# Two halves of a split weight, interleaved in one buffer instead of two buffers

## The chip, the cores and the metric

One core of a Trainium2 chip runs the whole program. The metric is the device time in microseconds, the median of several executions. TensorE multiplies, VectorE and ScalarE work element by element, GpSimd and SyncE here mostly issue transfers. A matmul on TensorE has a stationary operand, brought in by a separate weight load, and a moving operand that is streamed past it; both are read from SBUF, the on-chip memory of 128 partitions.

## What is computed

Two transformer blocks in a row on 256 positions of width 1024, all in fp32. The first has two kinds of attention and a gated feed-forward layer with a short convolution; the second has an attention layer and a gated convolution layer, each followed by a gated feed-forward layer. Cut to what matters here:

```python
# first block
h = rmsnorm(x, attn_norm_g[l]); proj = h @ w_in[l]
o_fox = fox_attention(...); o_sb = stick_breaking_attention(...)
x = x + o @ w_out[l]
h = rmsnorm(x, ffn_norm_g[l])
u = causal_dwconv(h @ w_up[l], conv_w[l], conv_b[l])
gate, val = jnp.split(u, 2, axis=-1)
x = x + (jax.nn.silu(gate) * val) @ w_down[l]
# second block, i = 0 and 1
mod = sc @ w_ada[i] + b_ada[i]
h = modulate(x, norm_mix[i], sh_m, sc_m)
y = moba_attention(h, w_qkv[j], w_o[j], ...) if i == 0 else short_conv(h, w_in[j], conv_w[j], w_out[j])
x = x + g_m[:, None, :] * y
h = modulate(x, norm_ffn[i], sh_f, sc_f)
x = x + g_f[:, None, :] * swiglu(h, w_gate_up[i], w_down[i])
```

Nearly all the arithmetic is in the products with weights: w_in, w_out, w_up, w_down, w_qkv_2, w_o_2, w_in_2, w_out_2 and two each of w_gate_up_2 and w_down_2.

## The kernel before

**Split products.** To keep fp32 accuracy with fast matmuls, every fp32 operand is split into two of type fp32r: an upper half (the rounded value) and a lower half (what the rounding left). A product is then three matmuls, in `products` (lines 1417, 1418, 1419): upper with upper, upper with lower, lower with upper.

**Chunks and units.** Weights arrive as 147 chunks of 1 MB (128 partitions x 2048 values), in a ring of four buffers `w_raw`, by transfers that SyncE issues. A chunk is two units of 128 x 1024 values (`UNIT`), 294 units in all. For each unit ScalarE copies the raw values to the upper half (`w_hi`, `split_unit`, line 505) and VectorE subtracts that from the raw values to give the lower half (`w_lo`, line 857). Both buffers are rings of `SPLIT` = 4 units. ScalarE may write unit u once TensorE is done with unit u - 4 (`unit_done`), VectorE once ScalarE is done (`hi_ready`), TensorE may use the unit once VectorE is done (`lo_ready`).

**Stages.** The chunks in order: IN1 (0 to 11), OUT1, UP1 (16 to 37), DOWN1 (38 to 48), QKV (49 to 60), OUT2, UP2 (65 to 86), DOWN2 (87 to 97), IN3 (98 to 109), OUT3, UP3 (114 to 135), DOWN3 (136 to 146). Between the units of IN1 and QKV stand the small matmuls of attention. UP and DOWN run mostly in hardware loops, and a loop of UP splits two chunks ahead, so the loop of UP3 also splits chunks 136 and 137.

**Which operand is stationary.** In most stages a 128 x 128 tile of the weights is stationary, and the activations (`act_hi`, `hid_hi`, `ot_hi`, ... with their lower halves) move, 256 columns at a time: a unit is 8 tiles, so 24 matmuls. In the chunks of the values (v) of both attentions, 2, 5, 10 and 11 of IN1 and 4, 7, 10 and 11 of QKV, the weights move, 256 columns at a time (`half_chunk` with `moving`). In DOWN3 (`down_tokens`) they move 512 columns at a time: a unit is 4 products, 12 matmuls.

**Beside the stream of weights**, VectorE adds up `ada_acc` (the product with w_ada_2, whose 48 MB come in over GpSimd's queue as `ada_raw`), does the convolutions, norms and residuals, and ScalarE does the activations. The order of work on each engine is written out by hand in the block of that engine; nothing reorders it.

Of the kernel before, what the change touches and what calls it, by code (L numbers as in the profile page):

```python
# [66 lines left out]

BANKS_DONE = {OUT1: 0, DOWN1: 1, OUT2: 4, DOWN2: 5, OUT3: 8, DOWN3: 9}
# [20 lines left out]
def model_kernel(nc, x, attn_norm_g, w_in, forget_bias, fox_out_g, sb_out_g, w_out, ffn_norm_g, w_up,  # L89
# [3 lines left out]
    with ctx:  # L93
# [8 lines left out]
        w_hi = sb("w_hi", [P, SPLIT, UNIT], F32R)  # L102
        w_lo = sb("w_lo", [P, SPLIT, UNIT], F32R)
# [224 lines left out]
        def unit(buf, u):  # L328
            return buf[:, u % SPLIT, :]
# [161 lines left out]
        def _(act):  # L491
# [5 lines left out]
            def split_unit(c, h, i=None):  # L497
                u = 2 * c + h
                if u == 0 and i is None:
                    act.wait_ge(w_first, 16)  # L500
                elif h == 0 or u == 1:
                    act.wait_ge(w_landed[c % RAW], at(16 * (c // RAW + 1), 16, i))
                if u >= SPLIT:
                    act.wait_ge(unit_done, at(u - SPLIT + 1, 8, i))
                act.activation(unit(w_hi, u), raw_half(c, h), ACT.Copy).then_inc(hi_ready, 1)  # L505
# [339 lines left out]
        def _(dve):  # L845
# [568 lines left out]
        def _(pe):  # L1414
# [6 lines left out]
            def half_chunk(c, h, dst, src_hi, src_lo, i=None, operand=None, moving=False):  # L1421
# [6 lines left out]
                whi, wlo = unit(w_hi, u), unit(w_lo, u)  # L1428
# [16 lines left out]
            def arriving(u, h, dst, src_hi, src_lo, operand):  # L1445

                for j in (2 * h, 2 * h + 1):
# [3 lines left out]
                    for k, t, w in tiles:  # L1451
                        o = dst[:, t * T:(t + 1) * T]
                        pe.matmul(o, unit(w_hi, u)[:, w], src_hi[:, k, :], start=k == 0 and t == 0, stop=False,  # L1453
                                  skip_group_check=True)
                        pe.matmul(o, unit(w_lo, u)[:, w], src_hi[:, k, :], start=False, stop=False, skip_group_check=True)  # L1455
                    pe.wait_ge(h_lo, 4 * operand + j + 1)
                    for k, t, w in tiles:
                        ins = pe.matmul(dst[:, t * T:(t + 1) * T], unit(w_hi, u)[:, w], src_lo[:, k, :], start=False,  # L1458
                                        stop=k == KT - 1, skip_group_check=True)
                ins.then_inc(unit_done, 1)  # L1460

            def first_half():
# [5 lines left out]
                for j in range(2):  # L1468
                    pe.wait_ge(h_hi, 2 * j + 2)
                    for k, t, o, w in tiles(j):  # L1470
                        pe.matmul(o, unit(w_hi, 0)[:, w], act_hi[:, k, :], start=k == 0 and t == 0, stop=False,
                                  skip_group_check=True)
                for j in range(2):
                    pe.wait_ge(h_lo, j + 1)
                    for k, t, o, w in tiles(j):
                        pe.matmul(o, unit(w_hi, 0)[:, w], act_lo[:, k, :], start=False, stop=False, skip_group_check=True)
                pe.wait_ge(lo_ready, 1)
                for j in range(2):
                    for k, t, o, w in tiles(j):
                        ins = pe.matmul(o, unit(w_lo, 0)[:, w], act_hi[:, k, :], start=False, stop=False,  # L1480
# [7 lines left out]
            def output_chunk(c0, n, h, k_hi, k_lo, ready=None):  # L1488
# [9 lines left out]
                for outputs in (range(4),) if n < 3 else (range(2), range(2, 4)):  # L1498
                    for r in tiles:
# [4 lines left out]
                        for o in outputs:  # L1504
                            w = slice(r % 2 * 2 * CW + o * P, r % 2 * 2 * CW + (o + 1) * P)
                            dst = bank[OUT_BANKS[c0][2 * (n % 2) + o // 2]][:, (o % 2) * T:(o % 2 + 1) * T]
                            ins = products(dst, unit(w_hi, w_unit)[:, w], unit(w_lo, w_unit)[:, w], k_hi(k), k_lo(k),
# [36 lines left out]
            def down_layer(c0, pair0):  # L1544
                def rows(d, i=None):
                    pe.wait_ge(hid_lo_r, at(pair0 + d + 1, 4, i))
                    for h in range(2):
# [3 lines left out]
                        for o in range(KT):  # L1551
                            w = slice(o * P, (o + 1) * P)
                            ins = products(bank[4 + o // 2][:, (o % 2) * T:(o % 2 + 1) * T], unit(w_hi, u)[:, w],
                                           unit(w_lo, u)[:, w], hid_hi[:, cols(kt, 8, i, 1), :], hid_lo[:, cols(kt, 8, i, 1), :],
# [10 lines left out]
                for j in range(4):  # L1565
                    for h in range(2):
                        u, kt = 2 * (c0 + 10) + h, 20 + h
                        for o in (2 * j, 2 * j + 1):
                            w = slice(o * P, (o + 1) * P)
                            ins = products(bank[4 + j][:, (o % 2) * T:(o % 2 + 1) * T], unit(w_hi, u)[:, w],  # L1570
                                           unit(w_lo, u)[:, w], hid_hi[:, kt, :], hid_lo[:, kt, :], False, h == 1)
# [381 lines left out]
```

## Time and profile before

| | before |
|---|---|
| median of the runs shown | 969.9 us (3 runs, 967.15 to 971.51) |
| profiled execution | 967.1 us, span of its profile 965.5 us, mean granted TensorE clock 0.996 |
| TensorE matmuls | 931.0 us busy, 7571 |
| TensorE weight loads | 904.0 us busy, 7571 |
| VectorE | 715.6 us busy |
| ScalarE | 482.4 us busy |
| GpSimd | 45.3 us busy |
| HBM read | 205.75 MB, 214 GB/s over the span |

Busy is the time in which an engine had an instruction under way. Matmuls are pipelined and their ends are modelled, so matmuls that follow each other overlap in the table, and a mean duration is longer than the time between two starts. Weight loads are listed as an engine of their own (PEld) and overlap the matmuls. Groups of instructions are named by line, engine, operation and by output and inputs: `bank<-act_hi,w_hi` has act_hi moving and w_hi stationary, `bank<-w_hi,act_hi` the other way round.

### The profile page before, as it was taken

The numbers are of one execution on the slowest core, as the hardware profiler recorded it, in microseconds if no ns is written. First come the engines' busy times: TensorE is split into PE (matmuls) and PEld (weight loads), VectorE is DVE, ScalarE is ACT, GpSimd is POOL, SyncE is SP. The second block draws the span as 40 slices with busy tenths as digits, with TensorE's granted clock in tenths as the row PEclk, the third lists the DMA queues.
The fourth block names the chain that finished last, engine by engine and source line by source line (L and its number), as shares of the span: only waits on it lengthen the run. The fifth ranks groups of instructions, "written<-read, shape, count | busy, mean of one in ns | idle before, by whom it ended". The sixth has DMA issues, their size and how long they took to land.

```text
span 965.5 us, 18807 instructions
## 1 busy us (share of the span) xinstructions
PE 931.0 (96%) x7571; PEld 904.0 (94%) x7571; DVE 715.6 (74%) x942; ACT 482.4 (50%) x704; POOL 45.3 (5%) x79
## 2 busy tenths in 40 slices
PE   7899899999999999999999999999999999999998
PEld 7899789999989999899999999999999999999886
DVE  6799757799999779988675777787867575555544
ACT  6345645566655336555464444534544454445541
POOL 4000000000010100001000001000000000000000
PEclk9999999999999999999999999999999999999999
DMA  9778332766767985566736788798465545656541
GB/s 296 236 270 316 113 129 69 240 217 218 228 253 286 382 289 175 177 216 220 240 114 212 253 278 297 266 367 282 134 210 181 175 131 183 209 176 208 173 140 44
DMA packets 130969, 207.61 MB, mean 215 GB/s; under 512 B 4582, under 2 KB 109408, under 8 KB 124768
## 3 DMA queue, kind: packets, MB, share of 16 engines
q1 hardware_dynamic: 122784, 156.43, 48.4%
q0 software_dynamic: 6912, 50.33, 14.5%
q8 instruction: 40, 0.66, 0.3%
q10 hardware_dynamic: 1216, 0.05, 0.1%
q14 instruction: 17, 0.14, 0.0%
HBM read 205.75 MB, written 1.05 MB: 214 GB/s over the span
## 4 chain that ended last, share of the span: by engine, by line
PE 64%; DVE 23%; ACT 4%; issue 4%; DMA 4%; ACTq 0%; POOL 0%; DVEq 0%; POOLq 0%
PE bank L1417 18%; PE bank L1418 18%; PE bank L1419 18%; DVE w_lo L857 8%; DVE ada_acc L872 4%; DVE conv L966 3%; DMA ada_raw<-in_w_ada 3%; ACT w_hi L505 2%; PE bank L1522 2%; PE bank L1458 1%; PE bank L1453 1%; PE bank L1455 1%; DVE hidden L979 1%; DVE scr L892 1%; PE bank L1637 1%
## 5 line engine op out<-in xcount | busy, mean ns | idle before, releaser
L857 DVE TENSOR_TENSOR w_lo<-w_raw,w_hi 128x1024 fp32r<-128x1024 f32 x294 | 354.0, 1223 | 152.9 <-ACT w_hi L505 149.7
L505 ACT ACTIVATE w_hi<-w_raw 128x1024 fp32r<-128x1024 f32 x294 | 306.0, 1055 | 250.3 <-PE bank L1419 240.8
L1417 PE MATMUL bank<-act_hi,w_hi 128*128 128x256 f32 x1440 | 401.3, 279 | 6.1 <-DVE w_lo L857 3.7
L1418 PE MATMUL bank<-act_lo,w_hi 128*128 128x256 f32 x1440 | 398.1, 276 | 0.0
L1419 PE MATMUL bank<-act_hi,w_lo 128*128 128x256 f32 x1440 | 398.1, 276 | 0.0
L1417 PEld LDWEIGHTS bank<-act_hi,w_hi 128*128 128x128 f32 x1440 | 270.4, 188 | 7.6 <-DVE w_lo L857 7.3
L1418 PEld LDWEIGHTS bank<-act_lo,w_hi 128*128 128x128 f32 x1440 | 270.5, 188 | 0.3 <-issue 0.2
L1419 PEld LDWEIGHTS bank<-act_hi,w_lo 128*128 128x128 f32 x1440 | 270.6, 188 | 0.0
L872 DVE SCALAR_TENSOR_TENSOR ada_acc<-ada_raw,silu_c,ada_acc 128x2048 f32<-128x2048 f32 x48 | 112.6, 2347 | 10.7 <-DMA ada_raw<-in_w_ada 10.7
L1417 PE MATMUL bank<-hid_hi,w_hi 128*128 (+1 forms) x352 | 98.2, 279 | 4.0 <-DVE w_lo L857 4.0
L1418 PE MATMUL bank<-hid_lo,w_hi 128*128 (+1 forms) x352 | 97.8, 278 | 0.0
L1419 PE MATMUL bank<-hid_hi,w_lo 128*128 (+1 forms) x352 | 97.8, 278 | 0.0
L1417 PEld LDWEIGHTS bank<-hid_hi,w_hi 128*128 128x128 f32 x352 | 66.6, 189 | 4.7 <-issue 4.7
L1418 PEld LDWEIGHTS bank<-hid_lo,w_hi 128*128 128x128 f32 x352 | 66.1, 188 | 0.0
L1419 PEld LDWEIGHTS bank<-hid_hi,w_lo 128*128 128x128 f32 x352 | 66.1, 188 | 0.0
L555 ACT ACTIVATE hid_hi<-hidden 128x512 f32 (+1 forms) x33 | 20.9, 632 | 70.5 <-DVE hidden L979 70.5
L459 POOL DMA_DIRECT2D ada_raw<-in_w_ada x48 | 25.5, 531 | 591.9 <-DVE ada_acc L872 576.0
L982 DVE TENSOR_TENSOR hid_lo<-hidden,hid_hi 128x512 f32 (+1 forms) x33 | 22.9, 693 | 28.9 <-ACT hid_hi L555 28.9
L1417 PE MATMUL bank<-w_hi,act_hi 128*128 128x256 f32 x128 | 38.3, 299 | 0.0
L1418 PE MATMUL bank<-w_lo,act_hi 128*128 128x256 f32 x128 | 36.8, 287 | 0.0
L1419 PE MATMUL bank<-w_hi,act_lo 128*128 128x256 f32 x128 | 36.6, 286 | 0.0
L1417 PE MATMUL bank<-ot_hi,w_hi 128*128 128x256 f32 x128 | 36.3, 283 | 0.0
(283 smaller groups left out, 1236.7 us busy)
## 6 DMA issues: line engine op xcount, KB each, us to landing
ada_raw<-in_w_ada POOLq DMA_DIRECT2D x48, 1024.0 KB, 5.5
w_raw<-in_w_gate_up SPq DMA_DIRECT2D x44, 1024.0 KB, 5.1
w_raw<-in_w_down SPq DMA_DIRECT2D x33, 1024.0 KB, 5.0
w_raw<-in_w_in SPq DMA_DIRECT2D x23, 1024.0 KB, 7.2
w_raw<-in_w_up SPq DMA_DIRECT2D x22, 1024.0 KB, 5.7
w_raw<-in_w_qkv SPq DMA_DIRECT2D x12, 1024.0 KB, 7.9
w_raw<-in_w_out SPq DMA_DIRECT2D x8, 1024.0 KB, 5.2
w_raw<-in_w_o SPq DMA_DIRECT2D x4, 1024.0 KB, 5.9
```

Source lines behind the costliest of these rows:

```text
L459: pool.dma_start(ada_raw[:, j, :], w_ada_2[l][cols(j * P, 2 * P, i, P), s * ADA_W:(s + 1) * ADA_W]).then_inc(ada_landed[j], 16)
L505: act.activation(unit(w_hi, u), raw_half(c, h), ACT.Copy).then_inc(hi_ready, 1)
L555: act.activation(hid_hi[:, cols(2 * p, 4, i, 2), :], hidden[:], ACT.Copy).then_inc(hid_hi_r, 1)
L857: dve.tensor_tensor(unit(w_lo, u), raw_half(c, h), unit(w_hi, u).bitcast(F32), ALU.subtract).then_inc(lo_ready, 1)
L872: dve.scalar_tensor_tensor(ada_acc[:, s, :], ada_raw[:, n % 2, :], silu_c[:, cols(k, ada_step[0], i, 1)], ada_acc[:, s, :], ALU.mult, ALU. ...
L892: dve.scalar_tensor_tensor(scr[:, k, :], res[:, k, :], gain(k), rstd[:], ALU.mult, ALU.mult).then_inc(hx_ready, 1)
L966: ins = dve.scalar_tensor_tensor(conv[:, q, lag:T], src[:, (q % 2) * T:(q % 2 + 1) * T - lag], vcol(tile, base + f, 4, i), conv[:, q, lag: ...
L982: dve.tensor_tensor(hid_lo[:, kt, :], hidden[:], hid_hi[:, kt, :].bitcast(F32), ALU.subtract).then_inc(hid_lo_r, 1)
L1417: pe.matmul(dst, a_hi, b_hi, start=start, stop=False, skip_group_check=True)
L1418: pe.matmul(dst, a_hi, b_lo, start=False, stop=False, skip_group_check=True)
L1419: return pe.matmul(dst, a_lo, b_hi, start=False, stop=stop, skip_group_check=True)
L1522: ins = pe.matmul(bank[SUM_BANK[n]][:, 0:T], w, scr[:, k, :], start=k == 0, stop=k == KT - 1)
```

## The change

One buffer `w_split` with room for both halves of four units takes the place of `w_hi` and `w_lo`; it has their total size, so no other buffer is moved. In a unit that is not in `MOVING` the two halves are interleaved value by value: upper 0, lower 0, upper 1, lower 1, and so on. Whoever writes or reads one half then uses a step of two values (8 bytes). In units of the chunks in `MOVING` the upper half takes the first 1024 values and the lower half the rest, each without a step. `MOVING` is the v chunks of IN1 and QKV and the chunks of DOWN3 from the third on: 17 chunks, 34 units. The first two chunks of DOWN3 are not in it. Every use of `unit(w_hi, ...)` and `unit(w_lo, ...)` becomes `unit(HI, ...)` and `unit(LO, ...)`. The number of instructions, their sizes, waits and order are the same on every engine. The core of the diff (the replacements in `arriving`, `first_half`, `output_chunk`, `down_layer` and the end of `down_tokens` are of the same kind as those shown):

```diff
@@ -65,6 +65,9 @@
 
 OUT_BANKS = {OUT1: (0, 1, 2, 3), OUT2: (0, 1, 2, 3), OUT3: (4, 5, 2, 3)}
 
+HI, LO = 0, 1
+MOVING = {2, 5, 10, 11} | {QKV + c for c in V_AT} | set(range(DOWN3 + 2, CHUNKS))
+
 BANKS_DONE = {OUT1: 0, DOWN1: 1, OUT2: 4, DOWN2: 5, OUT3: 8, DOWN3: 9}
 
 SH_M, SC_M, G_M, SH_F, SC_F, G_F = (KT * n for n in range(6))
...
@@ -99,8 +102,7 @@
 
 
         w_raw = sb("w_raw", [P, RAW, 2 * UNIT])
-        w_hi = sb("w_hi", [P, SPLIT, UNIT], F32R)
-        w_lo = sb("w_lo", [P, SPLIT, UNIT], F32R)
+        w_split = sb("w_split", [P, SPLIT, 2 * UNIT], F32R)
         res = sb("res", [P, KT, T])
         mod = sb("mod", [P, 2, 6 * KT])
         silu_c = sb("silu_c", [P, KT])
...
@@ -325,8 +327,12 @@
         stored = sem("stored")
 
 
-        def unit(buf, u):
-            return buf[:, u % SPLIT, :]
+        def unit(half, u):
+
+            both = w_split[:, u % SPLIT, :]
+            if u // 2 in MOVING:
+                return both[:, half * UNIT:(half + 1) * UNIT]
+            return both.rearrange("p (n two) -> p n two", two=2)[:, :, half]
 
         def raw_half(c, h):
             return w_raw[:, c % RAW, h * UNIT:(h + 1) * UNIT]
...
@@ -502,7 +508,7 @@
                     act.wait_ge(w_landed[c % RAW], at(16 * (c // RAW + 1), 16, i))
                 if u >= SPLIT:
                     act.wait_ge(unit_done, at(u - SPLIT + 1, 8, i))
-                act.activation(unit(w_hi, u), raw_half(c, h), ACT.Copy).then_inc(hi_ready, 1)
+                act.activation(unit(HI, u), raw_half(c, h), ACT.Copy).then_inc(hi_ready, 1)
 
             def squares(n, version):
                 for j in range(4):
...
@@ -854,7 +860,7 @@
             def split_unit(c, h, i=None):
                 u = 2 * c + h
                 dve.wait_ge(hi_ready, at(u + 1, 8, i))
-                dve.tensor_tensor(unit(w_lo, u), raw_half(c, h), unit(w_hi, u).bitcast(F32),
+                dve.tensor_tensor(unit(LO, u), raw_half(c, h), unit(HI, u).bitcast(F32),
                                   ALU.subtract).then_inc(lo_ready, 1)
 
             def split(c, i=None):
...
@@ -1425,7 +1431,7 @@
 
                 u = 2 * c + h
                 pe.wait_ge(lo_ready, at(u + 1, 8, i))
-                whi, wlo = unit(w_hi, u), unit(w_lo, u)
+                whi, wlo = unit(HI, u), unit(LO, u)
                 if operand is not None:
                     arriving(u, h, dst, src_hi, src_lo, operand)
                     return
...
@@ -1579,8 +1585,8 @@
                 def half_products(kt, u, j, first, last):
                     t, g = j // 2, slice(j % 2 * 512, (j % 2 + 1) * 512)
                     tok = slice(t * P, (t + 1) * P)
-                    return products(bank[4 + j][:, :], hid_hi[:, kt, tok], hid_lo[:, kt, tok], unit(w_hi, u)[:, g],
-                                    unit(w_lo, u)[:, g], first, last)
+                    return products(bank[4 + j][:, :], hid_hi[:, kt, tok], hid_lo[:, kt, tok], unit(HI, u)[:, g],
+                                    unit(LO, u)[:, g], first, last)
 
                 def rows(d):
                     pe.wait_ge(hid_lo_r, pair0 + d + 1)
```

## Rows read from the trace of the kernel before

**Rows 1.** The page: engines' shares of the span, and the chain that ended last.

```profile
PE 931.0 (96%) x7571; PEld 904.0 (94%) x7571; DVE 715.6 (74%) x942; ACT 482.4 (50%) x704; POOL 45.3 (5%) x79
...
PE 64%; DVE 23%; ACT 4%; issue 4%; DMA 4%; ACTq 0%; POOL 0%; DVEq 0%; POOLq 0%
PE bank L1417 18%; PE bank L1418 18%; PE bank L1419 18%; DVE w_lo L857 8%; DVE ada_acc L872 4%; DVE conv L966 3%; DMA ada_raw<-in_w_ada 3%; ACT w_hi L505 2%; PE bank L1522 2%; PE bank L1458 1%; PE bank L1453 1%; PE bank L1455 1%; DVE hidden L979 1%; DVE scr L892 1%; PE bank L1637 1%
```

**Rows 2.** Timeline near 500 us, TensorE and its loads: start us, duration us, engine, line.

```profile
500.02 0.28 PE L1418 MATMUL bank<-act_lo,w_hi 128*128 128x256 f32 x1
500.02 0.19 PEld L1419 LDWEIGHTS bank<-act_hi,w_lo 128*128 128x128 f32 x1
...
503.08 0.28 PE L1418 MATMUL bank<-act_lo,w_hi 128*128 128x256 f32 x1
```

**Rows 3.** Timeline near 218 us, TensorE, the same columns.

```profile
218.01 0.28 PE L1417 MATMUL bank<-act_hi,w_hi 128*128 128x256 f32 x1
...
221.54 0.28 PE L1417 MATMUL bank<-act_hi,w_hi 128*128 128x256 f32 x1
```

**Rows 4.** Table of stretches: stretch us, its length, busy (x instructions) of each engine, clock, DMA.

```profile
302.90:345.10 42.20, 42.20 (x360) 42.20 (x359) 35.32 (x24) 16.22 (x16) 5.52 (x8) 1.00 1.00 378
471.60:482.80 11.20, 11.20 (x97) 11.20 (x96) 7.93 (x13) 4.33 (x7) 0.53 (x1) 1.00 0.96 322
744.70:767.40 22.70, 22.70 (x194) 22.70 (x192) 13.51 (x16) 9.35 (x11) 0.00 (x0) 1.00 0.55 185
496.80:610.90 114.10, 114.10 (x1009) 114.10 (x1009) 81.05 (x73) 54.00 (x63) 5.52 (x8) 1.00 0.77 258
```

**Rows 5.** fp32 matmuls of 128 columns: two timeline rows, and groups by shape (busy, mean ns).

```profile
155.85 3.73 PE L1637 MATMUL bank<-ones,ada_acc 128*128 128x128 f32 x32
...
902.99 1.03 PE L1617 MATMUL bank<-ident,res 128*128 128x128 f32 x8
...
L1637 PE MATMUL bank<-ones,ada_acc 128*128 128x128 f32 x192 | 22.9, 275 | 0.0
...
L1637 PEld LDWEIGHTS bank<-ones,ada_acc 128*128 128x128 f32 x192 | 22.7, 192 | 0.4
...
L1617 PEld LDWEIGHTS bank<-ident,res 128*128 128x128 f32 x16 | 1.9, 141 | 0.3
```

**Rows 6.** Timeline: two of the moving weights (512 columns), and fp32 matmuls of 256 columns.

```profile
152.40 3.62 PE L1522 MATMUL bank<-scr,ones 128*128 128x256 f32 x16
...
898.18 0.39 PE L1417 MATMUL bank<-w_hi,hid_hi 128*128 128x512 f32 x1
...
902.30 0.39 PE L1417 MATMUL bank<-w_hi,hid_hi 128*128 128x512 f32 x1
```

**Rows 7.** Loads of 4 (step two), 8 and 128 columns: duration ns min/median/max; mean in the last.

```profile
L1698 PEld LDWEIGHTS bank<-upto,nlf x4: 82/86/87, 23.0 to 23.7; 128*4 128x4 f32 x4
...
L1417 PEld LDWEIGHTS bank<-act_hi,wf_hi x8: 85/88/88, 13.1 to 15.4; 128*8 128x8 f32 x8
...
L1417 PEld LDWEIGHTS bank<-act_hi,w_hi 128*128 128x128 f32 x1440 | 270.4, 188 | 7.6 <-DVE w_lo L857 7.3
```

**Rows 8.** The chain in order of time, first down projection: start us, us, what.

```profile
323.17 8.39 DMA ada_raw<-in_w_ada
```

**Rows 9.** The two splitting lines: duration ns min/median/max, first and last start us.

```profile
L857 DVE TENSOR_TENSOR w_lo<-w_raw,w_hi x294: 1203/1225/1228, 10.1 to 951.7; 128x1024 fp32r<-128x1024 f32 x147
...
L505 ACT ACTIVATE w_hi<-w_raw x294: 1037/1060/1109, 9.0 to 950.6; 128x1024 fp32r<-128x1024 f32 x147
```

**Rows 10.** Table of stretches, columns as in rows 4.

```profile
165.00:287.00 122.00, 116.98 (x1016) 115.80 (x1015) 107.84 (x152) 71.48 (x103) 4.99 (x7) 1.00 0.68 232
287.00:353.00 66.00, 63.36 (x532) 62.75 (x533) 56.45 (x47) 31.68 (x40) 7.10 (x11) 1.00 0.89 331
368.00:471.00 103.00, 98.98 (x786) 94.85 (x785) 87.47 (x148) 53.77 (x105) 5.52 (x8) 0.98 0.60 204
496.00:611.00 115.00, 115.00 (x1017) 115.00 (x1017) 81.85 (x73) 54.80 (x63) 5.52 (x8) 1.00 0.77 256
```

More of the change, by code:

```diff
@@ L1470, in first_half @@
                     for k, t, o, w in tiles(j):
-                        pe.matmul(o, unit(w_hi, 0)[:, w], act_hi[:, k, :], start=k == 0 and t == 0, stop=False,
+                        pe.matmul(o, unit(HI, 0)[:, w], act_hi[:, k, :], start=k == 0 and t == 0, stop=False,
                                   skip_group_check=True)
@@ L1475, in first_half @@
                     for k, t, o, w in tiles(j):
-                        pe.matmul(o, unit(w_hi, 0)[:, w], act_lo[:, k, :], start=False, stop=False, skip_group_check=True)
+                        pe.matmul(o, unit(HI, 0)[:, w], act_lo[:, k, :], start=False, stop=False, skip_group_check=True)
                 pe.wait_ge(lo_ready, 1)
@@ L1479, in first_half @@
                     for k, t, o, w in tiles(j):
-                        ins = pe.matmul(o, unit(w_lo, 0)[:, w], act_hi[:, k, :], start=False, stop=False,
+                        ins = pe.matmul(o, unit(LO, 0)[:, w], act_hi[:, k, :], start=False, stop=False,
                                         skip_group_check=True)
@@ L1506, in output_chunk @@
                             dst = bank[OUT_BANKS[c0][2 * (n % 2) + o // 2]][:, (o % 2) * T:(o % 2 + 1) * T]
-                            ins = products(dst, unit(w_hi, w_unit)[:, w], unit(w_lo, w_unit)[:, w], k_hi(k), k_lo(k),
+                            ins = products(dst, unit(HI, w_unit)[:, w], unit(LO, w_unit)[:, w], k_hi(k), k_lo(k),
                                            k == 0 and o % 2 == 0, k == KT - 1)
@@ L1552, in rows @@
                             w = slice(o * P, (o + 1) * P)
-                            ins = products(bank[4 + o // 2][:, (o % 2) * T:(o % 2 + 1) * T], unit(w_hi, u)[:, w],
-                                           unit(w_lo, u)[:, w], hid_hi[:, cols(kt, 8, i, 1), :], hid_lo[:, cols(kt, 8, i, 1), :],
+                            ins = products(bank[4 + o // 2][:, (o % 2) * T:(o % 2 + 1) * T], unit(HI, u)[:, w],
+                                           unit(LO, u)[:, w], hid_hi[:, cols(kt, 8, i, 1), :], hid_lo[:, cols(kt, 8, i, 1), :],
                                            kt == 0 and o % 2 == 0, False)
@@ L1569, in down_layer @@
                             w = slice(o * P, (o + 1) * P)
-                            ins = products(bank[4 + j][:, (o % 2) * T:(o % 2 + 1) * T], unit(w_hi, u)[:, w],
-                                           unit(w_lo, u)[:, w], hid_hi[:, kt, :], hid_lo[:, kt, :], False, h == 1)
+                            ins = products(bank[4 + j][:, (o % 2) * T:(o % 2 + 1) * T], unit(HI, u)[:, w],
+                                           unit(LO, u)[:, w], hid_hi[:, kt, :], hid_lo[:, kt, :], False, h == 1)
                         if j == 3:
```

6 lines of the change are left out of this document (3 added, 3 removed).

## The prediction

> **What bounds the kernel now.** Read the engines' shares first, then the chain that ended last [rows 1]. TensorE's matmuls are busy 931 of 965.5 us, its weight loads 904, VectorE 716, ScalarE 482. Matmul lines 1417 to 1419 alone hold 54% of the chain; the w_lo subtraction holds 8%. So the kernel's length is mostly the number of TensorE pairs (a 128x128 weight load and the matmul on it) times the time between two starts. Busy time and durations don't give that time, since pairs overlap: a matmul is shown with 0.28 us [rows 2]. Starts in the timeline do. In the second block's feed-forward layer 27 starts take 503.08 - 500.02 = 3.06 us, 113.3 ns each, and the load of the next pair starts in the same instant as a matmul [rows 2]. So a pair takes as long as the slower of one load and one matmul. In one step of the first up projection the same code takes 221.54 - 218.01 = 3.53 us for 30, 117.7 ns each [rows 3]. The table of stretches shows that this slower pace is kept in the first down projection (42.2 us for 360) and both output projections of the second block (97 in 11.2 and 194 in 22.7), against 1009 in 114.1 at the fast one [rows 4]. With that one step (about 95) and about 250 more in the attention stretches I estimate 1,000 of the pairs at about 118 ns, the others at 113.3.
>
> What does a pair consist of? A matmul of 256 fp32r columns at the full granted clock (2.4 GHz) has 106.7 ns of columns in it. Pairs whose matmul is fp32 on 128 columns are seen with two kinds of load. With an ordinary load 32 take 3.73 us; less the last one's 0.275, 31 gaps of 111.5 ns. With the shorter load of a transpose 8 take 1.03 us, 7 gaps of 108.3 ns when 0.27 is taken off likewise. The load durations are 192 and 141 ns [rows 5]. So 111.5 ns is the pace of an ordinary load, and both rates of the weight pairs lie 2 and 6.5 ns above it: something is lost when a load runs beside an fp32r matmul.
>
> **What the change touches.** The order of instructions on every engine is the same, and so are their number, sizes and waits; only addresses change. Of 294 units 260 are interleaved, 34 stay apart. Of the 260, 256 are loaded as stationary operand: 256 x 8 tiles x 3 products = 6,144 loads with a step of two. The other four (chunks 136 and 137, the first two of the last down projection) are split by the loop body of the up projection before, so they are interleaved although their weights move: 4 units x 4 x 3 = 48 matmuls of 512 columns read their moving operand with a step of two.
>
> **(a) The 48 moving reads.** They take 902.30 - 898.18 = 4.12 us for 18, 229 ns each, against 213.3 ns of columns at 2.4 GHz: already 7% over [rows 6]. An fp32 operand of 256 columns, read at half that pace, has 16 matmuls from 152.40 to 155.85, 216 ns each against 213.3, only 1% over [rows 5, 6]. So the fast stream is at the limit of what it can fetch. With a step of two it spans twice the memory. Bounds: nothing, and another 229 ns each, 48 x 0.229 = 11.0 us. I take 11.0, because the stream is over its columns before the change. TensorE is busy all through this stretch, so all of it lies on the path.
>
> **(b) The 6,144 loads.** A load now walks through 4 bytes in 0.83 ns (half the pace of an fp32r matmul's columns). With a step of two it walks through memory just as fast as the moving operand. Where both have one pace before (fp32 pairs, 111.5 ns), nothing is lost beyond the load's own time; where the paces differ, 2 to 7 ns are. That is the reason to expect a gain: two streams of one pace that get in each other's way once stay shifted. What it needs is that the step itself costs no time. The one row on that is small: loads of four columns with a step of two (nlf) take 82 ns at least and 87 at most, loads of eight adjacent columns 85 and 88 [rows 7]. From 8 to 128 columns the duration grows from 88 to 188 ns, 0.83 ns a column [rows 7], so four columns fewer should be 3.3 ns shorter: the least differ by 3, the most by 1. A doubled time per column would leave nothing of it. It speaks for a free step, though weakly.
> The pace after is bounded by 111.5 ns (the ordinary load remains) and 108.3 ns (the load falls out of the way) [rows 5]. The ordinary load is the nearer row, so I take 110.5. The first down projection gets nothing: its DMA share is 1.00 at 378 GB/s [rows 4], and the chain there waits for ada_raw transfers of up to 8.39 us [rows 8]. That leaves about 5,100 pairs at 113.3 and 600 at 118: 5,100 x 2.8 ns = 14.3 us and 600 x 7.5 ns = 4.5 us, together 18.8 us. At 111.5 it is 13.1 us, at 108.3 it is 31.3.
>
> **(c) The splitting.** ScalarE writes the upper half, VectorE reads it and writes the lower, both with a step of two. A unit costs 1.06 and 1.22 us now [rows 9]. No row has a step of one value on these engines. Bounds: nothing, and twice the time. I take nothing, since an fp32 value in 1.04 ns asks less of the memory than TensorE's 0.45 ns. The cover is VectorE's idle time: 14.2 us in the first up projection (107.84 of 122 busy, 44 units), so 0.32 us a unit; 15.5 us over 16 units in the qkv stretch; 33 us over 44 in the second up projection [rows 10]. ScalarE is about half busy there.
> The Trainium skill has two rules on this that disagree. "Vector Engine (DVE) Microarchitecture Reference", Measured stream behaviour on trn2, says that a port keeps its full rate only with runs of at least two adjacent 4-byte words, and gives 1.71 to 1.98 ns instead of 1.05 per column when single words hop; a step of two is not among its cases. By it a unit would need some 0.7 us more, and VectorE would be the bound in the up projections. "SBUF — State Buffer", Door 1, tells of 16-byte lines that need two hits each, which a step of two on fp32 still gives; by it both splitting and loads stay as they are. The row of four columns fits the second; no row of VectorE decides.
>
> **The sum.** Profiled execution 967.1 us (span 965.5). 967.1 - 18.8 + 11.0 = 959.3. The median of the runs shown, 969.9, lies 2.8 above the profiled execution; with that, 962.1 us. A measurement of this kernel can tell about 0.5% (4.8 us) from no change. By the bounds of (b) the same sum gives 967.8 and 949.6, and without the cost of (a) 938.6 at the best.
>
> **The rivals.**
> 1. Loads and matmuls keep their pace, the moving reads double: +11.0, 980.9. For it: fp32r matmuls of 512 columns are 7% over their columns although a load fills less than half of their time, so the 113.3 may be the matmul's own pace and no loss between streams. Against it: the same operands run at both 113.3 and 117.7. This is the case on the slower side; it decides from the point where (b) saves under 6 us, 1 ns a pair.
> 2. The load becomes the slower of the two. With a step of two it spans 1 KB, for which the fast matmul stream needs 113.3 ns; with the 4.8 ns that the ordinary load has over its 106.7 ns of columns, 118. Then 5,100 pairs lose 4.8 ns, 24.5 us, and with (a) it is 35.5: 1005. Against it: the row of four columns.
> 3. VectorE's pass with a step gets slower. It decides from 0.32 us a unit. At 0.6 us more: first up projection 107.84 + 26.4 = 134 against 122, +12; first down projection 56.45 + 13.2 = 69.7 against 66, +4 [rows 10]; attention and qkv about +4 together; with (a) and no gain in (b) +31: 1001. At twice the time it would be near +118: 1088.
> 4. A stepped load takes twice its time: 6,144 x 0.1 us = +614, with (a) 1595. Only the row of four columns speaks against it.
> 5. No difference anywhere (moving reads free too): 970.
>
> **Chances.** My forecast's case 0.48 (of it 0.08 within 0.5%), rival 1 0.20, rival 2 0.08, rival 3 0.12, rival 4 0.07, rival 5 0.05. From these: faster 0.40, same 0.15, slower 0.45 (a little of rival 1 counted as same). The single likeliest case is the gain, though losses together hold more. Its own range is 944 to 971. The range for eight in ten takes in rivals 1, 2 and 5 and the lower end of 3: 944 to 1010; rival 4 and the upper part of 3 stay outside.
>
> **What the profile after would show.** (b) right: starts in the up projections 110 to 111 ns apart, one pace in all stretches, the up projection's 114.1 us for 1009 pairs some 3 us shorter. Rival 1: 113.3 as before. Rival 2: about 118 everywhere, load durations over 188. Rival 4: load durations near 290. (a): the matmuls of chunks 136 and 137 about 457 ns apart, 229 from chunk 138 on. (c): w_lo still 1.22 us and w_hi 1.06. The forecast is wrong if the starts don't move, or if w_lo takes more than 1.5 us and TensorE waits for it.

## The result

| | before | after |
|---|---|---|
| median of the runs shown | 969.9 us (967.15 to 971.51) | 1010.7 us (3 runs, 1007.68 to 1011.28) |
| profiled execution | 967.1 us, span 965.5 | 1011.3 us, span 1009.7, mean granted clock 0.992 |

The change makes the kernel slower: the ratio of the times is 1.039, with a 95% interval of 1.030 to 1.048. The forecast of 962.1 us had the wrong sign, and the time lies 0.7 us above the upper end of the range. It is rival 2, to which I had given a chance of 0.08, that came out: the stepped weight load became the slower half of a pair.

### The profile page after: what moved, and what is told of

Read it like the earlier page. It is cut to its first block, busy times and chain, and to the rows that moved or that the text cites. A ratio compares the mean times of both kernels' runs of the same rounds, so it can differ in the third digit from the quotient of the medians.

```text
span 1009.7 us, 18807 instructions
## 1 busy us (share of the span) xinstructions
PE 979.6 (97%) x7571; PEld 943.2 (93%) x7571; DVE 716.9 (71%) x942; ACT 507.6 (50%) x704; POOL 45.4 (4%) x79
## 4 chain that ended last, share of the span: by engine, by line
PE 70%; DVE 17%; ACT 4%; DMA 4%; issue 4%; ACTq 0%; POOL 0%; DVEq 0%; POOLq 0%
PE bank L1425 21%; PE bank L1423 20%; PE bank L1424 20%; DVE w_split L863 5%; DMA ada_raw<-in_w_ada 4%; DVE ada_acc L878 4%; ACT w_split L511 2%; DVE conv L972 2%; PE bank L1528 2%; PE bank L1459 1%; PE bank L1464 1%; PE bank L1461 1%; DVE scr L898 1%; PE bank L1643 1%; DVE hidden L985 0%
## 5 line engine op out<-in xcount | busy, mean ns | idle before, releaser
L863 DVE TENSOR_TENSOR w_split<-w_raw,w_split 128x1024 fp32r<-128x1024 f32 x294 | 355.3, 1224 | 194.7 <-ACT w_split L511 193.4
L511 ACT ACTIVATE w_split<-w_raw 128x1024 fp32r<-128x1024 f32 x294 | 331.9, 1146 | 269.1 <-PE bank L1425 260.1
L1423 PE MATMUL bank<-act_hi,w_split 128*128 128x256 f32 x1440 | 408.5, 284 | 4.2 <-DVE act_lo L1246 2.5
L1425 PE MATMUL bank<-act_hi,w_split 128*128 128x256 f32 x1440 | 407.9, 283 | 0.0
L1424 PE MATMUL bank<-act_lo,w_split 128*128 128x256 f32 x1440 | 406.7, 282 | 0.0
L1423 PEld LDWEIGHTS bank<-act_hi,w_split 128*128 128x128 f32 x1440 | 281.0, 195 | 5.7 <-DVE w_split L863 5.4
L1424 PEld LDWEIGHTS bank<-act_lo,w_split 128*128 128x128 f32 x1440 | 280.6, 195 | 0.3 <-issue 0.2
L1425 PEld LDWEIGHTS bank<-act_hi,w_split 128*128 128x128 f32 x1440 | 279.3, 194 | 0.0
L1423 PE MATMUL bank<-hid_hi,w_split 128*128 (+1 forms) x352 | 100.2, 285 | 3.6 <-DVE w_split L863 3.6
L1424 PE MATMUL bank<-hid_lo,w_split 128*128 (+1 forms) x352 | 100.2, 285 | 0.0
L1425 PE MATMUL bank<-hid_hi,w_split 128*128 (+1 forms) x352 | 99.8, 284 | 0.0
L1423 PEld LDWEIGHTS bank<-hid_hi,w_split 128*128 128x128 f32 x352 | 69.2, 196 | 4.3 <-issue 4.3
L1425 PEld LDWEIGHTS bank<-hid_hi,w_split 128*128 128x128 f32 x352 | 69.0, 196 | 0.0
L561 ACT ACTIVATE hid_hi<-hidden 128x512 f32 (+1 forms) x33 | 20.9, 633 | 70.8 <-DVE hidden L985 70.8
L1423 PE MATMUL bank<-w_split,hid_hi 128*128 128x512 f32 x88 | 39.2, 445 | 0.0
L1424 PE MATMUL bank<-w_split,hid_hi 128*128 128x512 f32 x88 | 38.3, 435 | 0.0
```

The lines of the kernel that those rows point to most:

```text
L511: act.activation(unit(HI, u), raw_half(c, h), ACT.Copy).then_inc(hi_ready, 1)
L561: act.activation(hid_hi[:, cols(2 * p, 4, i, 2), :], hidden[:], ACT.Copy).then_inc(hid_hi_r, 1)
L863: dve.tensor_tensor(unit(LO, u), raw_half(c, h), unit(HI, u).bitcast(F32), ALU.subtract).then_inc(lo_ready, 1)
L1423: pe.matmul(dst, a_hi, b_hi, start=start, stop=False, skip_group_check=True)
L1424: pe.matmul(dst, a_hi, b_lo, start=False, stop=False, skip_group_check=True)
L1425: return pe.matmul(dst, a_lo, b_hi, start=False, stop=stop, skip_group_check=True)
```

## The profile after

First the page of the kernel after: shares of the span, the chain that ended last, and the two splitting groups (busy us, mean ns, idle time before them).

```profile
PE 979.6 (97%) x7571; PEld 943.2 (93%) x7571; DVE 716.9 (71%) x942; ACT 507.6 (50%) x704; POOL 45.4 (4%) x79
...
PE 70%; DVE 17%; ACT 4%; DMA 4%; issue 4%; ACTq 0%; POOL 0%; DVEq 0%; POOLq 0%
...
L863 DVE TENSOR_TENSOR w_split<-w_raw,w_split 128x1024 fp32r<-128x1024 f32 x294 | 355.3, 1224 | 194.7 <-ACT w_split L511 193.4
L511 ACT ACTIVATE w_split<-w_raw 128x1024 fp32r<-128x1024 f32 x294 | 331.9, 1146 | 269.1 <-PE bank L1425 260.1
```

Against [rows 1], TensorE has 49 us more of busy time for the same 7,571 matmuls, and its share of the chain goes from 64% to 70% while VectorE's falls from 23% to 17%. VectorE has as much work as before. So the time came from TensorE itself, and every other engine has only more slack. The distances between starts say where. Timeline of the kernel after in the last up projection (start us, duration, engine, line): 17 starts in 2.04 us.

```profile
849.88 0.28 PE L1423 MATMUL bank<-act_hi,w_split 128*128 128x256 f32 x1
...
851.92 0.28 PE L1425 MATMUL bank<-act_hi,w_split 128*128 128x256 f32 x1
```

That is 120.0 ns a pair, where [rows 2] had 113.3. The table of stretches (stretch, length, then busy time and instructions of PE, PEld, DVE, ACT, POOL, then clock, DMA share, GB/s) shows the same in every kind of stage: the first down projection, the first output projection of the second block, the second up projection, and the other output projection.

```profile
310.50:353.50 43.00, 43.00 (x360) 43.00 (x359) 34.29 (x23) 18.19 (x16) 5.53 (x8) 1.00 0.99 366
483.50:494.90 11.40, 11.40 (x96) 11.40 (x95) 7.99 (x13) 4.59 (x7) 0.53 (x1) 1.00 0.95 316
509.10:630.20 121.10, 121.10 (x1012) 121.10 (x1011) 81.41 (x73) 58.11 (x63) 5.53 (x8) 1.00 0.73 244
771.20:794.50 23.30, 23.30 (x195) 23.30 (x194) 13.12 (x17) 10.31 (x11) 0.00 (x0) 1.00 0.56 180
```

(An instruction that reaches over an edge is counted too, so length over count comes out some 0.3 ns low in the long ones and up to 3 ns low in those of a hundred.) The two paces of [rows 4] are gone: all stationary weights run at 120.0 ns, and at 121.1 in the output projection at 771 us. The granted clock is 1.00 in all of them, so no clock is in this. Over all starts of the two traces, distances over 150 ns left out, the mean distance of pairs with stationary weights goes from 114.40 to 120.08 ns. For 6,144 pairs that is 34.9 us. The pairs whose 256 weight columns move, which the change leaves without a step, stay as they were (117.3 and 116.9 ns).

Timeline of the last down projection of the kernel after, with 512 columns of weights moving: chunk 137 with a step, then chunk 138 without.

```profile
943.06 0.65 PE L1424 MATMUL bank<-w_split,hid_hi 128*128 128x512 f32 x1
...
953.03 0.65 PE L1425 MATMUL bank<-w_split,hid_lo 128*128 128x512 f32 x1
...
954.63 0.40 PE L1424 MATMUL bank<-w_split,hid_hi 128*128 128x512 f32 x1
...
955.79 0.39 PE L1423 MATMUL bank<-w_split,hid_hi 128*128 128x512 f32 x1
```

The first two rows are 22 starts in 9.97 us, 453 ns each; the last two 5 starts in 1.16 us, 232 ns each, against 229 in [rows 6]. So 48 matmuls at 453.5 instead of 229 cost 10.8 us.

Together 34.9 + 10.8 = 45.7 us, where the span grew by 44.2. Two smaller things of opposite sign make up the difference. The trace of the kernel after has two more stretches of 3.4 us at half the granted clock than that of the kernel before (clock, third from the end, in these rows):

```profile
144.30:147.70 3.40, 3.40 (x19) 3.40 (x18) 0.00 (x0) 0.35 (x1) 0.00 (x0) 0.50 0.68 240
355.90:359.30 3.40, 3.40 (x17) 3.40 (x18) 2.68 (x3) 0.00 (x0) 0.00 (x0) 0.50 1.03 347
```

In each some 16 pairs stand about 210 ns apart instead of 120, which costs 3 us in the two. Against that, the distances over 150 ns behind pairs with stationary weights, mostly waits, hold 3.9 us less than before; the waits for VectorE are part of it (7.7 us before TensorE's matmuls, now 5.3). So 3 us of the 44.2 are clock and not step. The run of 1007.68 us, whose mean clock was 0.996 as in the profile before, leaves 1007.68 - 967.1 = 40.6 us for the change, against 34.9 + 10.8 - 3.9 = 41.8 us by this account.

The loads and the splitting, durations in ns (a group's mean, or min/median/max):

```profile
L1423 PEld LDWEIGHTS bank<-act_hi,w_split 128*128 128x128 f32 x1440 | 281.0, 195 | 5.7 <-DVE w_split L863 5.4 <-issue 0.2
...
L863 DVE TENSOR_TENSOR w_split<-w_raw,w_split x294: 1208/1226/1231, 10.6 to 995.9; 128x1024 fp32r<-128x1024 f32 x147
...
L511 ACT ACTIVATE w_split<-w_raw x294: 1042/1158/1224, 9.4 to 994.8; 128x1024 fp32r<-128x1024 f32 x147
```

A load takes 195 ns where [rows 7] had 188. VectorE's subtraction is as it was (1226 against 1225 in [rows 9]), ScalarE's copy is slower at the median by 0.10 us (1158 against 1060). VectorE's wait for that copy grew from 149.7 to 193.4 us. That looks alarming and is not: the growth of 43.7 us is the growth of the span (44.2) with VectorE's work unchanged. It waits longer because TensorE frees the units later.

## The experiments

Two explanations were open for the slower pairs. One is the step. The other is the place: the single buffer also puts the halves at other addresses, and [rows 2, 3] show that pairs of one kind run at 113.3 or 117.7 ns for a reason not yet known. For the step in turn there were three theories. **Theory A**: a load with a step of two takes longer by itself. **Theory B**: its wider reach hinders the matmul beside it. **Theory C**: the stepped writes of ScalarE and VectorE hinder TensorE's reads.

### e1_all_apart: one buffer, no step anywhere

```diff
-MOVING = {2, 5, 10, 11} | {QKV + c for c in V_AT} | set(range(DOWN3 + 2, CHUNKS))
+MOVING = set(range(CHUNKS))
```

> Keeps the one buffer w_split, but no unit is interleaved (every chunk in MOVING), so only addresses differ from before. If the step of two is the cause, this runs like the kernel before: 970 us, starts 113.3 or 117.7 ns apart, w_hi copy 1.06 us. If instead the loss came from where the halves lie (both halves of a unit now within 8 KB), it stays near 1000 us with starts near 120 ns.

Measured 973.41 us against 972.67 for the kernel before on the same chip, ratio 1.000 (0.997 to 1.003). The buffer's place costs nothing that can be seen (0.3%); the step does it all. The mean distance is 115.04 ns, a mixture like that of the kernel before (114.40). Table of stretches of this run, first down projection and last up projection:

```profile
308.60:341.20 32.60, 32.60 (x289) 32.54 (x288) 27.45 (x19) 13.09 (x13) 3.28 (x7) 1.00 1.00 375
793.10:907.40 114.30, 114.30 (x1011) 114.30 (x1010) 66.03 (x65) 54.77 (x63) 0.00 (x0) 1.00 0.60 197
```

The first of these ran at 117.8 ns in the kernel before [rows 4]; here 32.6 us for 289 is 112.8, by its starts 113.4. In exchange the input projection ahead of the last output projection ran at 117.8 here and at 113.3 before.

### e2_up3_down3_apart and e4_up3_down3_only: the change in one part

e2 is the kernel after with the step taken out of the last up and down projection; e4 has it only there.

```diff
 # e2
-MOVING = {2, 5, 10, 11} | {QKV + c for c in V_AT} | set(range(DOWN3 + 2, CHUNKS))
+MOVING = {2, 5, 10, 11} | {QKV + c for c in V_AT} | set(range(UP3, CHUNKS))
 # e4
+MOVING = set(range(CHUNKS)) - set(range(UP3, DOWN3 + 2))
```

> As the changed kernel, but the last up projection and the whole last down projection are apart. By the sum of pairs: 48 moving reads give back 48 x 0.224 = 10.8 us, and 44 units x 24 pairs x (120.1 - 113.3) ns = 7.2 us: 1010.7 - 18 = 992.7 us. If the step of the moving reads cost nothing and the pairs are slow for another reason than the step, it stays near 1010.

> The opposite of the second experiment: only the last up projection and the first two chunks of the last down projection are interleaved, every other unit is apart. If the parts simply add, before 972 + 10.8 (48 moving reads) + 44 x 24 x 6.7 ns (7.1 us) = 990 us, a ratio of 1.018. If the pairs of the other stages were slow only because of what came before them, it would come out another way.

Measured: e2 987.62 against 972.67, ratio 1.018 (1.014 to 1.023); e4 994.0 against 976.58 of its own chip, ratio 1.018 (1.011 to 1.025). Last up projection of e2:

```profile
801.80:916.20 114.40, 114.40 (x1011) 114.40 (x1010) 66.02 (x65) 54.77 (x63) 0.00 (x0) 1.00 0.60 197
```

It is back at 113.3 ns where the kernel after had 120.0, all 512-column matmuls of e2 are at 229.6, and its other stages stay at 120.0. In e4 it is the other way round: 120.0 in the last up projection, 48 matmuls at 453, and the old mixture elsewhere. The two ratios, 1.8% and 1.8%, add up to the 3.9% of the whole within their intervals. So the cost is local: each unit pays for itself where TensorE reads it, and nothing is seen to be handed on to a later stage. I had expected 18 us back from e2; by the ratios (3.9% less 1.8%) it is some 20, the same within the interval. A little of that is clock: three of the four runs of e2 had a mean clock of 0.998 or 1.000, the kernel before beside it 0.989 to 0.996.

### p1_probe: each engine's access by itself

This kernel computes nothing of the reference (nor do p2 and p3): it runs blocks of 48 or 96 pairs on made-up data with one thing changed between blocks, and the same ScalarE and VectorE instructions as the splitting, with one step changed at a time.

```diff
 # st(s, half, t): tile t of the upper or lower half, values s apart
-pe.matmul(bank[0][...256 columns], st((1, 1)[half], half, t), (a_hi, a_lo)[m][...256 columns], ...)
+pe.matmul(bank[0][...256 columns], st((2, 2)[half], half, t), (a_hi, a_lo)[m][...256 columns], ...)
```

Other blocks have a step of three or four, or 8, 128 or 512 columns.

> Computes nothing of the reference, it only measures: blocks of 48 pairs of a weight load and an fp32r matmul with other engines idle, loads with a step of 1, 2, 3 and 4 values, moving operands of 8, 128, 256 and 512 columns; then ScalarE copies and VectorE subtractions of 128x1024 with steps of 1, 2 and 4; then blocks of pairs beside stepped writes of ScalarE or VectorE. Theory A, a stepped load is slower by itself and becomes the slower half of a pair: with 8 moving columns step 1 gives 111 ns and step 2 118 to 120, with 256 columns 113 and 120, with 512 columns 229 both; step 4 about 220 whatever the columns. Theory B, the load loses time only against the moving stream: with 8 columns both steps 111 ns, with 256 columns 113 and 120, with 512 step 2 over 229. Theory C, the loss comes from ScalarE's stepped writes: alone 113 with both steps, beside stepped writes 120. ScalarE's copy with a stepped output 1.15 us instead of 1.06 under all, VectorE 1.22 with steps of 1 and 2 and more with 4.

The TensorE part was half spoiled by the clock. Share of the granted clock in 40 slices of this run:

```profile
PEclk9999955557999758599999965555555555999999
```

It fell to half in the sixth slice (at 45.1 us), in the first block of 8-column matmuls, and in those slices a load took 330 ns and a pair 213 both with adjacent values and with a step of two, so several blocks say nothing. What ran at the full clock was unexpected: pairs of 256 columns took 120.0 ns with a step of one *and* with a step of two. Here the step costs nothing, but at a pace that the kernel before never has. fp32 pairs of 128 columns took 111.7 ns without a step, as in [rows 5] (111.5), and 117.8 with it, which speaks for theory A. Where 256 moving columns and the load both had a step of two, a pair took 229.0 ns: the stepped moving read costs the same here as in chunks 136 and 137, about twice its time.

The other engines gave clean rows. Duration ns min/median/max, no work on TensorE beside them: ScalarE's copy of 1024 values without a step, with the output in steps of two, and of four; VectorE's subtraction without a step, with upper half and output in steps of two, and both in steps of four.

```profile
L76 ACT ACTIVATE s_act<-raw x8: 1039/1039/1056, 199.4 to 206.1; 128x1024 fp32r<-128x1024 f32 x8
...
L79 ACT ACTIVATE s_act<-raw x8: 1091/1092/1099, 207.0 to 214.0; 128x1024 fp32r<-128x1024 f32 x8
...
L85 ACT ACTIVATE s_act<-raw x8: 2029/2052/2061, 223.0 to 235.5; 128x1024 fp32r<-128x1024 f32 x8
...
L105 DVE TENSOR_TENSOR s_dve<-raw,w x8: 1219/1220/1225, 237.6 to 245.6; 128x1024 fp32r<-128x1024 f32 x8
...
L114 DVE TENSOR_TENSOR s_dve<-raw,w x8: 1228/1229/1230, 264.9 to 272.8; 128x1024 fp32r<-128x1024 f32 x8
...
L117 DVE TENSOR_TENSOR s_dve<-raw,w x8: 1999/2020/2029, 273.9 to 287.2; 128x1024 fp32r<-128x1024 f32 x8
```

A step of two costs VectorE 0.7% and ScalarE 5% (1042 against 1128 ns, 8%, while TensorE ran its pairs beside it, where the kernel has 1060 against 1158, 9%). A step of four costs VectorE 1.7 times and ScalarE twice the time. In the three blocks in which ScalarE or VectorE wrote with a step beside pairs, the pairs stayed at 120.0 ns, as in the one with adjacent writes. That alone doesn't refute theory C, since these pairs were at the slow pace from the start. p3_probe does: there the pace goes from 113.7 to 120.1 ns with no other engine at work.

### p2_probe: the load alone, and what surrounds it

```diff
-pe.matmul(bank[0][...8 columns], st((1, 1)[half], half, t), (a_hi, a_lo)[m][...8 columns], ...)
+pe.matmul(bank[0][...8 columns], st((2, 2)[half], half, t), (a_hi, a_lo)[m][...8 columns], ...)
```

> Computes nothing of the reference, it only measures pairs with all other engines idle; short blocks stand behind long ones so that the granted clock stays full. In the first probe fp32 pairs of 128 columns took 111.7 ns with step 1 and 117.7 with step 2, which speaks for a load slower by itself. Theory A (load slower by itself, set by the 16-byte pieces it touches): 8 moving columns give 111.5 ns at step 1, 117 to 118 at step 2, about 174 at step 3 and 233 at step 4; with 192 columns 111.5 and 118 to 120; with 320 and 512 columns both steps alike (load hidden). Theory B (loss only against the moving stream): 8 columns 111.5 at both steps 1 and 2, and 192 columns nearer to 111.5 than to 120 at step 2. In the first probe step 1 with 256 columns also ran at 120: the blocks with one thing changed (kernel's own order, two banks, new operand every tile, a fresh sum every time, moving operand shifted by 4 to 128 values) tell which of them makes 120 out of 113.3. With only the lower half's loads stepped, theory A gives a triple between 3 x 113.3 and 3 x 120.

Here the 8-column matmuls, beside which the load sets the pace, come in short blocks between long ones. The edit is the step of `w` alone (lines 95, 105, 115, 125: one to four). Loads of this run, durations in ns and first and last start of each block of 24, and then the timeline's last start of the first two:

```profile
L95 PEld LDWEIGHTS bank<-a_hi,w x16: 188/192/192, 43.2 to 45.8; 128*128 128x128 f32 x16
...
L105 PEld LDWEIGHTS bank<-a_hi,w x16: 196/196/198, 53.2 to 55.9; 128*128 128x128 f32 x16
...
L115 PEld LDWEIGHTS bank<-a_hi,w x16: 253/263/266, 63.2 to 67.3; 128*128 128x128 f32 x16
...
L125 PEld LDWEIGHTS bank<-a_hi,w x16: 310/330/330, 74.7 to 80.0; 128*128 128x128 f32 x16
```

```profile
43.25 0.19 PEld L95 LDWEIGHTS bank<-a_hi,w 128*128 128x128 f32 x1
...
45.82 0.19 PEld L95 LDWEIGHTS bank<-a_hi,w 128*128 128x128 f32 x1
...
53.16 0.20 PEld L105 LDWEIGHTS bank<-a_hi,w 128*128 128x128 f32 x1
...
55.87 0.20 PEld L105 LDWEIGHTS bank<-a_hi,w 128*128 128x128 f32 x1
```

23 gaps of 2.57 / 23 = 111.7 ns with a step of one, 2.71 / 23 = 117.8 with two. By the same reading a step of three gives 4.03 / 23 = 175.2 and a step of four 5.35 / 23 = 232.6 (the granted clock fell to half at 77.8 us, in the second half of this block, with no change in its pace). That is theory A: the stepped load is slower with almost no matmul beside it, and slower by itself than a whole pair at 113.3. From a step of two on the time grows by the memory spanned, 57 ns for each further unit of step (that is 512 bytes more over the load). A step of one is not half of a step of two, since there something else, some 111.5 ns, is the limit. With 192 columns, where the load still sets the pace, it is 111.7 ns without a step and 118.9 with it, as theory A had it.

Theory B has a part too. With 512 columns, where a load has more than twice the time it needs, pairs took 227.2 ns without a step (10.68 us for 47) and 233.2 with it (10.96): a hidden load slowed the matmul by 6 ns. With 320 columns there was no difference (147.0 and 146.8). Theory A had both alike. With 256 columns, blocks in which only the lower or only the upper half's loads had a step ran at 119.1 and 119.8 ns; they decide nothing, since the block without a step was already at 120.0.

```profile
184.75 0.40 PE L215 MATMUL bank<-a_hi,w 128*128 128x512 f32 x1
...
195.43 0.39 PE L215 MATMUL bank<-a_hi,w 128*128 128x512 f32 x1
...
195.66 0.39 PE L220 MATMUL bank<-a_hi,w 128*128 128x512 f32 x1
...
206.62 0.40 PE L220 MATMUL bank<-a_hi,w 128*128 128x512 f32 x1
```

The probe's own riddle was why 256-column pairs took 120.0 ns without a step. Another output bank, a new activation tile and a new sum at each pair changed nothing (120.0 each). Starting the moving operand 4, 8, 16 or 32 values later did: 118.9, 116.7, 117.9 and 118.7 ns. At 64 it was 119.8, at 128 again 120.0.

### p3_probe: the same pairs with the operands placed as in the kernel

In the kernel before `act_hi` lies 48 values past a multiple of 64 (64 values are 256 bytes). 112 is 48 past 64. So this probe repeats the pairs with the moving operand 112 values on, and with fifteen other shifts.

```diff
-pe.matmul(..., (a_hi, a_lo)[m][:, 0 + (t // 2) * 256:0 + (t // 2) * 256 + 256], ...)
+pe.matmul(..., (a_hi, a_lo)[m][:, 112 + (t // 2) * 256:112 + (t // 2) * 256 + 256], ...)
```

> Computes nothing of the reference, it only measures pairs of a load and a matmul of 256 fp32r columns, other engines idle, with the moving operands shifted against the weights; in the real kernel act_hi starts 112 values past a multiple of 1 KB. If the shift decides between 113.3 and 120 for step 1, the blocks at 112 values give 113.3 (or 117.7) with step 1 and 120 with step 2, as in the kernel. If the shift has nothing to do with it, all blocks of step 1 give 120 as the unshifted one did. Stepped loads at other shifts: never under 117.7, the pace of the stepped load alone; if one gives 113.3, the load's own pace is not the limit. The scan over step 1 may show a shift with less than 113.3, which would be worth trying in the kernel.

Timeline, first and last start of the blocks without a step, with two, and without again, all at shift 112:

```profile
32.26 0.29 PE L85 MATMUL bank<-a_hi,w 128*128 128x256 f32 x1
...
40.33 0.28 PE L85 MATMUL bank<-a_hi,w 128*128 128x256 f32 x1
40.44 0.28 PE L90 MATMUL bank<-a_hi,w 128*128 128x256 f32 x1
...
48.97 0.28 PE L90 MATMUL bank<-a_hi,w 128*128 128x256 f32 x1
49.09 0.28 PE L95 MATMUL bank<-a_hi,w 128*128 128x256 f32 x1
...
57.14 0.28 PE L95 MATMUL bank<-a_hi,w 128*128 128x256 f32 x1
```

71 gaps: 8.07 us, 8.53 us and 8.05 us, or 113.7, 120.1 and 113.4 ns. The kernel's own numbers came back in a program with nothing else in it. Shift 48 gave 113.6. Each other shift without a step was between 116.7 and 120.0, and a shift and the one 64 values on gave the same (8 and 72: 116.7; 24 and 88: 120.0; 40 and 104: 117.3). The hope of a place under 113.3 did not come true. With a step of two the six shifts tried gave 120.0 to 121.7. So without a step the pace here depends on where the moving operand stands modulo 256 bytes, with 113.4 the best and 120.0 the worst, and the step puts every pair at the worst or a little beyond. Only the moving operand was shifted, and the weights' tiles stayed on multiples of 64 values. Whether its place counts by itself or against the place of the stationary operand is therefore not shown.

### k2_ot_shift64: using that in the kernel before

By this the output projections should reach 113.3 as well, if `ot_hi` (32 past a multiple of 64) stood at 48 past one. The gap ahead of it is made 48 values smaller, which does that:

```diff
-        ot_shift_by = sb("ot_shift_by", [P, 112], stack=phase)
+        ot_shift_by = sb("ot_shift_by", [P, 64], stack=phase)
```

> The kernel before with one number changed: the gap ahead of ot_hi is 64 values instead of 112, so that ot_hi and ot_lo start 48 values past a multiple of 64, as act_hi does, instead of 32. In the probe 48 (and 112) gave 113.3 ns a pair and 32 gave 118.4, with the same sequence of five that the output projections of the kernel before show. If the shift acts in the real kernel as in the probe, the 384 pairs on ot go from 118.6 to 113.3 ns: -2 us, 0.2%, visible in the trace, too small for the runs. If not, they stay at 118.6.

Table of stretches of this run, the two output projections and the last up projection:

```profile
476.10:486.80 10.70, 10.70 (x97) 10.70 (x96) 7.94 (x13) 4.15 (x6) 0.53 (x1) 1.00 0.99 333
748.70:770.40 21.70, 21.70 (x194) 21.70 (x193) 13.50 (x16) 9.22 (x10) 0.00 (x0) 1.00 0.60 191
786.30:905.00 118.70, 118.70 (x1010) 118.70 (x1009) 65.93 (x65) 54.62 (x63) 0.00 (x0) 1.00 0.58 190
```

Against [rows 4] the same 97 and 194 pairs take 10.7 and 21.7 us instead of 11.2 and 22.7: the placement does what the probe said. The time is 968.38 us against 971.51, ratio 0.998 (0.995 to 1.000). Some 2 us of 970 can't be told from no change here, and the third row shows one reason: in this execution the last up projection ran at 117.8 ns, with the same code and the same place of `act_hi` and the weights as in the kernel before, where it ran at 113.3:

```profile
784.00:898.50 114.50, 114.50 (x1008) 114.34 (x1008) 65.40 (x63) 54.94 (x63) 0.00 (x0) 1.00 0.61 200
```

Which of the two paces a whole stretch takes changes from one kernel's profile to the next, and what picks it stays open. The place is not all of it: in e1 the last output projection ran at 120.0 ns without any step, where the kernel before had 118.7 at the same places modulo 256 bytes.

## Why the prediction was wrong

**What bounds the kernel** was right: TensorE's starts, one pair after another, and little else on the way. So was reading the pace from starts and not from durations: the starts' distances, the two stretches at half the clock and the shorter waits account for the growth of the span within 1 us.

**(a), the moving reads, was right**: 11.0 us expected, 10.8 measured, 453 ns a matmul where I had written 457.

**(b), the loads, is the step that failed**: a gain of 18.8 us was expected, and a loss of 34.9 came. The sum put the step's own cost for a load at nothing, and the load set the pace. Three things were wrong in it.
First, the evidence for a free step. The four-column loads of [rows 7] were asked to show whether a step of two costs time. Over 128 columns it costs 188 to 195 or 196 ns in duration and 111.7 to 117.8 ns in pace, 0.05 ns a column. Over four columns that is 0.2 ns, and the rows are read to one. They could rule out a doubling (rival 4), and they did; they could not tell a gain from rival 2. I set the chances as if they spoke against both.
Second, the lower bound of the pace. I took 111.5 ns, "the pace of an ordinary load", for one that walks through twice the memory. It was the price of a load without a step. The measured one is 117.8 on the fp32 pairs, already above the 113.3 that it was to improve.
Third, the idea that two streams of one pace get out of each other's way. They do settle in one steady pattern, as expected: one pace in all stages, where there had been two. But it is a slow one, 120.0 ns or more at every placement tried, and not the fastest.

**Rival 2 had the mechanism and most of the size.** It had said 118 ns for a load that spans 1 KB, and measured are 117.8 almost alone and 120.0 in a pair. Its working holds beyond this one number: it gives 1.5 x 113.3 + 4.8 = 174.8 ns for a step of three and 2 x 113.3 + 4.8 = 231.4 for four, where p2_probe has 175.2 and 232.6. Its 24.5 us became 34.9 as follows: 6,144 x (117.8 - 114.4) = 20.9 us is what the load alone asks for, and 6,144 x (120.1 - 117.8) = 14.1 us comes on top in the pair, which neither rival nor forecast had. That the load alone is too slow is shown (p1, p2); why the pair then adds 2.3 ns is not. Theory B's 6 ns with 512 columns may be of the same kind.
The Trainium skill's "SBUF — State Buffer" says in Door 1 and in its specifications that a 16-byte line needs at least two hits for full bandwidth. That rule stood behind the guess that a step of two on fp32 is free. It holds for VectorE here within 0.7%, and gives 5% too little for ScalarE's copy and for TensorE's load. For TensorE's moving read it fails: with a step of two that takes 453 ns instead of 229. Beyond a step of two the runs agree that fewer than two hits a line cost time: 57 ns for 512 more bytes spanned is 1.8 ns for each 16. They do not agree with the same note in Door 1 where it counts four fp32 values as free to stride.

**The first down projection** was to get nothing, being bound by DMA (share 1.00). It went from 117.8 to 120.0 ns a pair with a DMA share of 0.99, and e1 ran its long steady stretch at 113.4 with a share of 1.00. A full DMA share was no limit of TensorE there. In that stretch of e1 ScalarE, which splits the weights first, waited 18.0 us for TensorE to free units, and no wait of it for a transfer of weights is seen; the ada_raw transfers of [rows 8] held up VectorE alone.

**(c), the splitting, was right in its sum**, though ScalarE's part was not free: 0.10 us a unit at the median, 0.09 in the mean. ScalarE is half idle, and TensorE's waits for VectorE did not grow (5.3 us against 7.7). Of the two rules that I had set side by side, the trace decides against the one of "Vector Engine (DVE) Microarchitecture Reference", Measured stream behaviour, for this case: VectorE keeps its rate at a step of two (1229 against 1220 ns). At four it takes 2020 ns for 1024 columns, 1.97 ns each with the fixed time in it, and there it agrees with the 1.71 to 1.98 of that section. Rival 3, which rested on a slower VectorE, is out.

**The chances.** 0.08 for rival 2 was too little. Its reasoning was made of rows (a stream over 1 KB takes 113.3 ns, a load adds 4.8), the forecast's was an idea without a row, and the single row against rival 2 could not have seen it. Read that way, both would have had about the same chance, and the forecast's sign should have been "slower".

## What to carry to other kernels

Before a row is used as evidence that something is free, work out what it would show if it were not: four columns of an effect of 0.05 ns a column can't be seen. Where TensorE runs back to back, keep the values of both of its operands adjacent in memory, those of the stationary one too, although its load seems hidden behind the matmul. If a layout has to be interleaved, let the engine with slack do the stepping: a step of two costs VectorE 0.7% and ScalarE 5 to 9%, a step of four 1.7 times and twice the time.

## What the runs showed that I had not expected

- A pair of an ordinary load and a 256-column fp32r matmul takes 113.4 to 120.0 ns by the place of the moving operand modulo 64 values (p2, p3). In the kernel before, the output projections ran at 118.7 ns, and the later one went to 113.3 when its moving operand was put where the probe was fastest (k2). "TensorE: Matmul & The Clock Gate" of the Trainium skill, under Step-by-step, says that loading the next tile doesn't take read bandwidth from the running matmul, as each has its own port. The runs don't agree: a stepped load that is fully hidden behind 512 columns adds 6 ns to 227. Whether the effect of the place has to do with the load too is not shown.
- From a step of two on, TensorE's load (57 ns for 512 bytes more), TensorE's moving read (453 ns over 4 KB), ScalarE (2050 ns over 16 KB) and VectorE (2020 over 16 KB, with fixed time) all come near 1.8 to 2 ns for each 16 bytes spanned. At a step of two ScalarE and VectorE are above this by their own pace, and TensorE is not. That fits with the same step being nearly free on the two slow engines and costly on the fast one; it is a reading of these few points, and no run tests it further.
- With the same code and operands at the same places a stretch of 1,000 pairs ran at 113.3 ns in one kernel's profile and at 117.8 in another's (last up projection: kernel before and k2). It moves the time by some 4.5 us, and it is still open what picks the pace.
